# Mixing stage of a two-layer kernel with its GpSimd work on the other engines, value parts between groups of scores, and attention's output panel as split parts

## What is computed

```python
proj = h @ w_in                                  # q, k, v, z, xbc, dt
a = softmax(q1 k1 + bias) - lam * softmax(q2 k2 + bias)   # 8 heads, two maps each, causal
o = rms_norm(a @ v, subln_g) * (1.0 - lambda_init)
xbc = silu(causal_depthwise_conv(xbc, conv_w, conv_b))
dt = softplus(dt + dt_bias); a = -exp(a_log)
y = ssd_chunked(xs * dt[..., None], a * dt, bm, cm)       # 2 chunks of 128 tokens, 16 heads
y = y + xs * d_skip
y = rms_norm(y * silu(z), norm_g)                # 2 groups
mixed = concatenate([o, y]) @ w_out              # 512 + 1024 rows
x = x + rms_norm(mixed, mix_post_g)
```

## Time and profile before

| what | us |
|---|---|
| median of 3 runs | 1694.07 (1692.89 to 1694.5) |
| profiled execution | 1692.44 |
| its span, first to last instruction | 1690.7 |
| TensorE busy | 1582.9 (94%) |
| VectorE busy | 1235.1 (73%) |
| ScalarE busy | 795.9 (47%) |
| GpSimd busy | 155.4 (9%) |
| mean granted TensorE clock | 0.971 |

### The profile page before, as it was taken

One profiled execution on the slowest core, in us unless ns is written; L12 is line 12 of the kernel. 1 busy time (PEld: TensorE's weight loads), 2 busy tenths in 40 slices (PEclk: granted clock), 3 DMA queues, 4 the chain that ended last, 5 costly groups with the idle time before them and its releaser, 6 DMA issues.

```text
span 1690.7 us, 25985 instructions
## 1 busy us (share of the span) xinstructions
PE 1582.9 (94%) x9080; PEld 1363.3 (81%) x9080; DVE 1235.1 (73%) x2038; ACT 795.9 (47%) x1212; POOL 155.4 (9%) x85
## 2 busy tenths in 40 slices
PE   6989889989999999999999999799997988879997
PEld 5777778879998888878888888688877967568886
DVE  4575559999998777677777777677777685367776
ACT  4544345447776343344444444544445653254443
POOL 1000257860000000000000000000001200000000
PEclk9999999999999999999999999899997989889999
DMA  5444334532324555555555555355552322345552
GB/s 199 175 147 171 131 125 163 187 125 100 115 108 151 197 198 189 183 174 199 180 192 191 183 196 198 137 191 189 183 194 78 139 75 100 125 139 196 185 187 99
DMA packets 38952, 270.40 MB, mean 160 GB/s; under 512 B 4705, under 2 KB 5217, under 8 KB 6642
## 3 DMA queue, kind: packets, MB, share of 16 engines
q1 hardware_dynamic: 37296, 266.97, 44.2%
q10 hardware_dynamic: 1602, 2.71, 0.5%
HBM read 268.62 MB, written 1.05 MB: 160 GB/s over the span
## 4 chain that ended last, share of the span: by engine, by line
PE 80%; DVE 15%; ACT 3%; issue 1%; DMA 1%; DVEq 0%; SPq 0%; ACTq 0%
PE ps L696 47%; PE ps L731 17%; PE ps L733 7%; PE ps L943 3%; DVE arena L1857 2%; PE ps L685 1%; DVE wlo L525 1%; PE ps L730 1%; DVE arena L1835 1%; PE ps L802 1%; DVE arena L1815 1%; DVE arena L1818 1%; DVE arena L1824 1%; DVE arena L1812 1%; DVE arena L1821 1%
## 5 line engine op out<-in xcount | busy, mean ns | idle before, releaser
L731 PE MATMUL ps<-XT,whi 128*128 128x512 f32 x1200 | 430.9, 399 | 1.9 <-DVE wlo L525 1.9
L696 PE MATMUL ps<-XT,whi 128*128 128x256 f32 x1696 | 315.6, 305 | 4.2 <-DVE wlo L525 4.2
L733 PE MATMUL ps<-XT,wlo 128*128 128x256 f32 x1050 | 295.6, 281 | 0.0
L504 ACT ACTIVATE whi<-raw 128x1024 fp32r<-128x1024 f32 x178 | 187.3, 1058 | 221.6 <-PE ps L696 161.2
L525 DVE TENSOR_TENSOR wlo<-raw,whi 128x1024 fp32r<-128x1024 f32 x146 | 186.5, 1289 | 121.5 <-ACT whi L504 120.2
L696 PE MATMUL ps<-whi,HAh 128*128 128x512 f32 x688 | 269.7, 392 | 5.5 <-DVE HAl L1943 3.0
L696 PEld LDWEIGHTS ps<-XT,whi 128*128 128x128 f32 x1696 | 268.0, 196 | 4.6 <-issue 4.6
L696 PE MATMUL ps<-wlo,HAh 128*128 128x512 f32 x688 | 268.8, 391 | 0.0
L696 PE MATMUL ps<-whi,HAl 128*128 128x512 f32 x688 | 268.3, 390 | 0.0
L731 PEld LDWEIGHTS ps<-XT,whi 128*128 128x128 f32 x1200 | 223.8, 189 | 47.4 <-DVE wlo L525 2.2
L733 PEld LDWEIGHTS ps<-XT,wlo 128*128 128x128 f32 x1050 | 199.6, 190 | 5.9
(11 more groups left out here) (267 smaller groups left out, 2104.1 us busy)
## 6 DMA issues: line engine op xcount, KB each, us to landing
raw<-in_experts SPq DMA_DIRECT2D x128, 1024.0 KB, 4.7
raw<-in_panels SPq DMA_DIRECT2D x58, 1024.0 KB, 4.8
raw<-in_ffa SPq DMA_DIRECT2D x33, 1024.0 KB, 4.8
raw<-in_ffb SPq DMA_DIRECT2D x33, 1024.0 KB, 4.8
arena<-in_row_post ACTq DMA_DIRECT2D x3, 512.0 KB, 3.7
X<-in_x SPq DMA_DIRECT2D x2, 512.0 KB, 5.3
out<-X SPq DMA_DIRECT2D x2, 512.0 KB, 2.7
arena<-in_row_ln ACTq DMA_DIRECT2D x2, 256.0 KB, 7.5
```

What stands on the lines that cost most here:

```text
L504: act.activation(whi[:, buf(p), :], half(item_of(p), p % 2), ACT.Copy).then_inc(part_hi, 1)
L696: last = pe.matmul(out, x if w_moving else w, w if w_moving else x, start=start and n == 0, stop=stop and n == 2)
L731: last = pe.matmul(out, wh[:, k], XT[:, k], start=k == 0, stop=k == NK - 1)
L733: pe.matmul(out[:, T:], wl[:, k], XTh[:, k], start=False, stop=False)
```

## The change

- **Retrieval.** GpSimd makes remainders only up to part S_EXP+23 (POOLED = 24). The remaining 10 are VectorE's, one after each fourth L1857 and one after each side's sums; before the two sides VectorE waits for GpSimd's last. TensorE's loop over these parts is written out from part 24.
- **Mixing without GpSimd.** The differences TA are 32 copies 128x128 on ScalarE: four in each round of the convolution loop, 16 between the two groups of decays. The step sizes enter in `weights`, now 16 SCALAR_TENSOR_TENSOR 128x128 a chunk instead of two TENSOR_TENSOR 128x1024, and TensorE multiplies with XS instead of XD. The skip enters when yd is read: 8 instructions 128x64 a bank instead of one of 128x512. XDS is VectorE's.
- **Earlier split.** Part S_XB+4 is split after conv_first(0) on ScalarE and before conv(0) on VectorE.
- **Value parts.** TensorE does one value part after each group of four scores. av0 and av1, and later wm0 and wm1, have banks of their own (4 and 5). The use table moves with it, so at4 to at7 are read with one more part split ahead, and so on.
- **Order after the gates.** yd2 and yd3 come after ao, yo after the transposes of ao. ScalarE squares ao straight from PSUM, VectorE sums each tile and scales it straight from PSUM.
- **Output panel.** Attention's 512 rows of w_out are four split parts (wm has 12 parts now) with activations split in two (stream "att"), instead of the raw panel. The weights' DMAs stay the same.
- **Table load.** warm_root(3) stands after the gates' read-outs instead of before the last squares.

The core of the diff:

```diff
+POOLED = 24
...
-_use(*[(f"at{i}", "dve") for i in range(16)])
-_by_token("av0", "av1", "act")
+for _r in range(4):
+    _use(*[(f"at{i}", "dve") for i in range(4 * _r, 4 * _r + 4)])
+    _part(main="av1" if _r == 3 else None)
+_use(("av0", "act"), ("av1", "act"))
 _by_token("zz0", "zz1", "act")
 _by_token("zz2", "zz3", "act")
-_use(*[(f"yd{i}", "dve") for i in range(4)], ("st0", "act"), ("st1", "act"), ("yo0", "dve"), ("yo1", "dve"),
-     ("ao0", "dve"), ("ao1", "dve"))
+_use(("yd0", "dve"), ("yd1", "dve"), ("st0", "act"), ("st1", "act"), ("ao0", "dve"), ("ao1", "dve"), ("yd2", "dve"),
+     ("yd3", "dve"), ("yo0", "dve"), ("yo1", "dve"))
 assert _parts == S_WM
-_wide("wm", 8)
+_wide("wm", 12)
...
+OWN_BANK = {"av0": 4, "av1": 5, "wm0": 4, "wm1": 5}
+MAIN_BANK, _n = [], 0
+for _name, _ in MAIN:
+    MAIN_BANK.append(OWN_BANK.get(_name, _n % 4))
+    _n += _name not in OWN_BANK
...
-            return S_WQ <= p < S_G
+            return S_WQ <= p < S_EXP + POOLED
...
-            for p in range(S_WQ, S_G):
+            for p in range(S_WQ, S_EXP + POOLED):
...
-            pool.wait_ge(pool_const2, 9)
-            pool.wait_ge(ad_ready, 1)
-            for c in range(2):
-                pool.tensor_tensor(TA[c], MGT.unsqueeze(1).broadcast_to([P, SSM_H, P]),
-                                   AD[:, c, :].unsqueeze(2).broadcast_to([P, SSM_H, P]), ALU.mult)\
-                    .then_inc(ta_ready, 1)
-
-            t_read_all(pool, "xs", 4)
-            for c in range(2):
-                xs = XS[:, c, :].rearrange("p (h n) -> p h n", h=SSM_H)
-                pool.tensor_tensor(XD[:, c, :].rearrange("p (h n) -> p h n", h=SSM_H), xs,
-                                   DT[:, c, :].unsqueeze(2).broadcast_to([P, SSM_H, SSM_P]), ALU.mult)\
-                    .then_inc(xd_ready, 1)
-            pool.wait_ge(xd_ready, 2)
-            for c in range(2):
-                xs = XS[:, c, :].rearrange("p (h n) -> p h n", h=SSM_H)
-                pool.tensor_tensor(xs, xs, SMALL[:, 2, :].unsqueeze(2).broadcast_to([P, SSM_H, SSM_P]), ALU.mult)\
-                    .then_inc(xskip_ready, 1)
-
-            read_out(pool, "cum")
-            pool.tensor_tensor(XDS.rearrange("p (h n) -> p h n", h=SSM_H),
-                               XD[:, 0, :].rearrange("p (h n) -> p h n", h=SSM_H),
-                               ECUM[:, 2, :].unsqueeze(2).broadcast_to([P, SSM_H, SSM_P]), ALU.mult)\
-                .then_inc(xds_ready, 1)
...
+                if g == 3:
+                    token_part(["av0", "av1"], S_AV, r)
...
-            pe.wait_ge(xd_ready, 2)
-            for c in range(2):
+            def within_tokens(c):
+
                 pe.wait_ge(w_ready, 2 * c + 2)
                 for g in range(2):
                     name = f"yd{2 * c + g}"
...
                     for j in range(8):
                         h = 8 * g + j
                         last = pe.matmul(bank(name)[:, SSM_P * j:SSM_P * j + SSM_P], W[c][:, h, :],
-                                         XD[:, c, SSM_P * h:SSM_P * h + SSM_P], start=True, stop=True)
+                                         XS[:, c, SSM_P * h:SSM_P * h + SSM_P], start=True, stop=True)
                     last.then_inc(main_done, 1)
 
+            within_tokens(0)
...
+            within_tokens(1)
             pe.wait_ge(att_y, 1)
             transposes("att", tiles(AOUT, 4))
-
-            t_read_all(pe, "att", 2)
+            read_out(pe, "st1")
+            for g in range(2):
+                claim(pe, f"yo{g}")
+                pe.matmul(bank(f"yo{g}"), XBC[:, 10 + g, P:T], SSTATE[:, g, :], start=True,
+                          stop=True).then_inc(main_done, 1)
             names = [f"wm{i}" for i in range(4)]
-            raw_panel(names, [RAW2, RAW2 + 1], [MIXA[:, k] for k in range(4)])
+            new_stream("att")
+            wide_panel(names, S_WM, range(4), claims=True, ends=False)
             pe.wait_ge(ssm_y, 1)
             transposes("ssm", tiles(XS, NK))
             new_stream("ssm")
-            wide_panel(names, S_WM, range(NK), start=False)
+            wide_panel(names, S_WM + 4, range(NK), start=False)
...
+            def differences(c, heads):
+
+                for h in heads:
+                    last = act.activation(TA[c][:, h, :], MGT, ACT.Copy, scale=AD[:, c, h:h + 1])
+                if h == SSM_H - 1:
+                    last.then_inc(ta_ready, 1)
...
             conv_first(0)
+            split_to(S_XB + 4)
...
+            act.wait_ge(ad_ready, 1)
             for j in range(2, 6):
                 conv_first(j)
                 conv_act(j - 2)
+                differences(0, range(4 * j - 8, 4 * j - 4))
...
             decays(0)
+            differences(1, range(SSM_H))
             decays(1)
+            split_to(S_AV + 1)
...
-                split_to(S_AV + r + 1)
+                split_to(S_AV + r + 2)
...
+            warm_root(3)
...
+            for tt in range(NT):
+                b = take(f"ao{tt}")
+                act.activation(ASQ[:, tt, :], b, ACT.Square).then_inc(att_sq, 1)
             head_root(2, 16)
-            turned("att", 2, MIXA, lambda k: col("subln"))
+            ssm_squares(0)
+            stream_hi("att")
+            ssm_squares(1)
             head_root(3, 4)
...
-            warm_root(3)
             norm_stats(8, *products_of("fb"))
...
+            dve.wait_ge(part_lo, S_EXP + POOLED)
...
+                    if j % 4 == 3:
+                        split_to(S_EXP + POOLED + 5 * side + j // 4)
...
+                split_to(S_EXP + POOLED + 5 * side + 4)
             dve.wait_ge(pool_const, 1)
             dve.tensor_copy(iota, IOTA)
-            dve.wait_ge(part_lo, S_G)
...
+            split_to(S_XB + 4)
             conv(0)
+            split_to(S_XB + 5)
...
-                for g in range(2):
-                    w = W[c][:, 8 * g:8 * g + 8, :]
-                    dve.tensor_tensor(w, w, CB[:, 2 * c + g, :].unsqueeze(1).broadcast_to([P, 8, P]), ALU.mult)\
-                       .then_inc(w_ready, 1)
+                for h in range(SSM_H):
+                    w = W[c][:, h, :]
+                    ins = dve.scalar_tensor_tensor(w, w, DT[:, c, h:h + 1], CB[:, 2 * c + h // 8, :], ALU.mult, ALU.mult)
+                    if h % 8 == 7:
+                        ins.then_inc(w_ready, 1)
...
+            split_to(S_ZZ + 1)
             for r in range(4):
-                split_to(S_AV + 1 + r)
                 normalise(r)
-            take("yd0")
-
-            dve.wait_ge(xskip_ready, 2)
-            for i in range(4):
+                split_to(S_ZZ + 2 + r)
+            read_out(dve, "cum")
+            link(dve.tensor_tensor(SMALL[:, 0, :], DT[:, 0, :], ECUM[:, 2, :], ALU.mult))
+            dve.tensor_tensor(XDS.rearrange("p (h n) -> p h n", h=SSM_H), XS[:, 0, :].rearrange("p (h n) -> p h n", h=SSM_H),
+                              SMALL[:, 0, :].unsqueeze(2).broadcast_to([P, SSM_H, SSM_P]), ALU.mult)\
+               .then_inc(xds_ready, 1)
+
+            def within_tokens(i):
+
+                b = take(f"yd{i}")
                 c, g = i // 2, i % 2
-                b = take(f"yd{i}")
-                y = XS[:, c, 512 * g:512 * g + 512]
-                read_done(dve.tensor_tensor(y, y, b, ALU.add))
-                if i == 1:
-                    after("yd1")
-                    after("zz3")
-                    dve.tensor_tensor(XS[:, 0, :], XS[:, 0, :], Z[:, 0, :], ALU.mult).then_inc(ssm_gated, 1)
+                for j in range(8):
+                    h = 8 * g + j
+                    y = XS[:, c, SSM_P * h:SSM_P * h + SSM_P]
+                    ins = dve.scalar_tensor_tensor(y, y, SMALL[:, 2, h:h + 1], b[:, SSM_P * j:SSM_P * j + SSM_P],
+                                                   ALU.mult, ALU.add)
+                read_done(ins)
+
+            dve.wait_ge(xds_ready, 1)
+            within_tokens(0)
+            within_tokens(1)
...
+                dve.wait_ge(att_sq, tt + 1)
+                ins = dve.tensor_reduce(hst[:, 2 % 2, 0, 8 * tt:8 * tt + 8],
+                                        ASQ[:, tt, :].rearrange("p (h v) -> p h v", h=AT_H), AX, ALU.add)
+            link(ins)
+            rs = head_scale(2, 16, AT_V, 1.0 - LAMBDA_INIT)
+            for tt in range(NT):
+                b = take(f"ao{tt}")
+                ins = dve.tensor_tensor(AOUT[:, tt, :].rearrange("p (h v) -> p h v", h=AT_H),
+                                        b.rearrange("p (h v) -> p h v", h=AT_H),
+                                        rs[:, 8 * tt:8 * tt + 8].unsqueeze(2).broadcast_to([P, AT_H, AT_V]), ALU.mult)
+                read_done(ins)
+            after("ao1")
+            dve.sem_inc(att_y, 1)
+            within_tokens(2)
+            stream_lo("att")
+            within_tokens(3)
...
-                read_done(dve.tensor_copy(AOUT[:, tt, :], b))
-            after("ao1")
-            link(dve.tensor_tensor(ASQ, AOUT, AOUT, ALU.mult))
```

(23 more changed lines are left out.)

99 lines of the change are left out of this document (39 added, 60 removed).

## The result

The change made the kernel slower: median 1703.35 us (1702.12 to 1707.8, 4 runs) against 1694.28 before, ratio 1.0058, 95% interval 1.0045 to 1.0072. The forecast was 1696.1 with a range up to 1702. The span of the profiled execution went from 1690.7 to 1700.4, by +9.7 where I had +2.0.

| stage, us | before | after | difference | forecast |
|---|---|---|---|---|
| start to the mixing stage's first transposes | 1273.5 | 1267.8 | −5.7 | −3.9 |
| to the end of the first group's maxima | 93.8 | 98.4 | +4.6 | −0.9 |
| to the end of the last gate part | 46.5 | 59.1 | +12.6 | +12.2 |
| to the first part of the state-space output | 48.5 | 44.6 | −3.9 | −6.3 |
| to the end | 228.4 | 230.5 | +2.1 | +0.8 |

A forecast was written before the change was run, and what follows sets the result against it. TensorE was taken as the bound, carrying 80% of the chain that ended last. Terms −3.9 − 0.9 + 12.2 − 6.3 + 0.8 gave +2.0 before rounding, on the median of 1694.07 1696.1; range 1689 to 1702.

The forecast's parts named there:

- First block: Selection in the first block: TensorE restarts at 376.0 instead of 379.85, −3.9 us.
- the option I had priced at 1.3 and not taken: First block: the clock does not fall behind TensorE's restart, another −1.3 us, left out of the sum.
- Mixing up to the first maxima: Start of mixing to first group's maxima: stall and slow clock go, −7.2; ScalarE's differences and weights add 6.3; sum −0.9.
- The rule that I set against the weights: Mixing: 58 + N cycles at 0.96 GHz, so 16 small instructions take 3.1 us, term +0.7 for +1.9; not followed.
- the clock as a rival: TensorE's clock stays low in scores and gate parts or falls again in the output panel: +4.4 us, 1700.5, chance 0.22.
- a clock other than 1.00 in the gate parts: Gate parts: one of the listed signs that the forecast is wrong; it expected a clock of 1.00 there.
- Scores to the end of the gates: Attention's scores to last gate part: a group costs 9.5 us instead of 3.7, end at +58.7 against 46.5, +12.2.
- side by side: Scores: remainders not held by the exponentials, TensorE ends at about +42, 16.7 less than forecast, 1679.4, chance 0.08.
- Gates to the state-space output: Last gate part to first state-space output part: 42.2 us against 48.5, −6.3; split parts for the raw panel give −5.6.
- End: End of the program: a table load of 1.28 now stands behind the last square, root starts 0.8 later, +0.8 us.
- The figure of 2.66 us for a switch: End: the skill's table load cost with a drain; by it the term would be +2.2, not +0.8; not followed.
- slower at 0.40: Chance of a slower kernel: 0.10 from the forecast's own spread, 0.22 clock, 0.08 late remainders in the first block.

The follow-up runs named there:

- three delayed forms: The kernel before with two, four or six dummy VectorE instructions ahead of the mixing stage, each executed once: spans 1697.1, 1697.8 and 1691.8 (unchanged 1691.3).
- the selection's edit: The kernel before with the retrieval's edit alone (GpSimd stops at part 24, ten remainders on VectorE): 1693.7, ratio 0.9994.

## Why the prediction was wrong

**First block, right in its place.** 376.00 forecast, 376.00 found; what was late next was ScalarE's exponential, as said. But the stage gained 5.7 for 3.9. 1.9 of it is the clock, which rose sooner behind the restart (mean 0.91 over 372 to 390, not 0.72): the option I had priced at 1.3 and not taken. This error goes the other way and hides 1.8 us of the miss.

**Mixing up to the first maxima, the step that failed: −0.9 forecast, +4.6 found.** The waits were sized well (a copy on ScalarE took 0.30, the weights 4.20; at the start of the convolution TensorE waited 0.81 + 0.22 for 1.2, the four copies ahead of the transposes took 1.16 for 1.2, the wait ahead of the rounded part was 1.9 for 2.0). The step that failed is that the sum carried full clock behind all of them. Instead the rows showed 5.20 for 3.67 at the decays, 2.55 + 1.09 for the ten transposes and the sums ahead of them (1.14 + 0.41 + 0.58 before), and 7.48 for 5.76 at aq: 4.8 us behind the two longer waits, and with the differences moved the rows are back at full speed. Another 1.0 was in the first stretch, 10.25 for 9.25, which no edit touches: it took 10.25 to 10.33 in seven of the eight profiles of the changed kernel and its edits and 9.20 in the eighth, and 9.25 to 10.24 in the six others. The rule that I set against the weights (the Trainium skill, VectorE: DVE Perf Modes, The TRN2 errata: 3.1 us for 16 small instructions, an estimate from its figure) doesn't hold here, 4.20 measured, and that section of the Trainium skill says itself that the figure comes out too short for a single instruction. I named the clock as a rival, but put it in the scores' and gates' stretch and in the output panel. In the scores and the first gate parts it was low (a part of 4.59 for 2.76; 0.50 from 1400.8 to 1406, though I had named a clock other than 1.00 in the gate parts as a sign of being wrong), but that cost nothing: VectorE and ScalarE set the pace, and the last three parts ran at 1.00. In the output panel it cost 1.9.

**Scores to the end of the gates, right.** 12.2 forecast, 12.6 found; maxima 9.56 apart for 9.5, normalisation 34.5 after the first maxima as worked out; the run with the rounding moved takes 17.2 of it back, against 16.7 worked out for the rival "side by side".

**Gates to the state-space output, mechanism right, size off.** The wait ahead of the fourth part was 2.80 for 2.9; that part then took 4.62 for 2.76, the clock again, and on the path of the next rounding too. −3.9 for −6.3. The terms that I wrote out add to 42.0, not 42.2, so my own figure should have been −6.5.

**End.** 0.5 for the table load, for 0.8, and some 1.5 that I had not in the sum: the clock behind two sets of transposes (0.6 in the output panel's last parts, 0.9 in the second feed-forward). The root did start 0.8 later, but before, VectorE's last product (L1636, 1684.08 to 1684.76) had covered 0.2 to 0.3 of it. The figure of 2.66 us for a switch (the Trainium skill, ScalarE: Activation LUTs, What ACT_TABLE_LOAD costs) isn't borne out here either: load at 1692.84, root at 1694.14.

**The chances.** The clock case stood at 0.22 with 1700.5, and slower at 0.40. The sign was not excluded; the sum's likeliest value was low because every pause that the change makes behind the first block was priced at its own length.

## What to carry to other kernels

A rounding, a copy or any step that other engines wait for belongs ahead of a wait in its engine's program, not behind it: one line's place was 17 us here, and turned the same change from 0.6% slower into 0.4% faster. Where TensorE is the bound, price a new pause of 2 to 3 us above its own length, since the work behind it may run at half clock: here one of 2.80 us brought 1.9 of slow work, one of 1.9 brought 1.7, and moving 2.3 us of waits away brought 6.9. And before a gain of some 3 us is believed, look whether untouched stages have changed their time between the two profiles.

## What the hardware showed that I had not expected

TensorE's granted clock fell behind some waits and not behind others of the same length. The decays of the kernel before, of its three delayed forms and of the one with the selection's edit, behind waits of 1.73 and 0.44 us in all six, took 3.67 in four of them, 5.13 in one and 6.31 in one. At the program's start, two projections that no kernel here changes took 8.46 us each in some executions and 10.0 in others (both slow in those with two and four instructions of delay, spans 1697.1 and 1697.8; both fast in the one with six, 1691.8). One and the same program varies with the clock: 19 executions of the kernel before lie between 1689.87 (mean clock 0.973) and 1698.89 (0.968), and of the ten of the selection's edit the lower heap has 0.971 or 0.972 and the upper 0.968. That is more than many edits are worth. Which stages are slow in the upper heap wasn't profiled. What decides the fall stays open: the runs show that it isn't the length of the wait right ahead alone, and that the clock some 20 us earlier differed too in the two slow cases. Whether a shift of the start by a microsecond does it, or a chance of each execution, they don't show.
